# Alternating the first feed forward's up and down slabs, seven block products in 14 of 16 down slabs, weight sums on GpSimd

## The reference, cut to what matters

```python
u = rmsnorm(h, norm_ff_g) @ w1              # (256, 1024) @ (1024, 4096)
h = h + jnp.square(jax.nn.relu(u)) @ w2     # (256, 4096) @ (4096, 1024)
```

## Time and profile before

| What | Value |
|---|---|
| median of 3 runs | 883.88 us (883.88 to 883.88) |
| profiled execution | 884.08 us, span 882.2 us |
| PE busy | 874.6 us, 99% of the span |
| VectorE, ScalarE, GpSimd busy | 647.6, 502.4, 117.9 us |
| granted clock of PE over the span | 1.00 (full speed) |
| HBM read | 158.86 MB, 181 GB/s over the span |

### The profile page before, as it was taken

The page is one execution under the profiler, slowest core; times in us unless marked ns, Lnnn a source line. Parts: engine busy times, 40 slices in busy tenths (PEclk is TensorE's granted clock), DMA queues, the critical chain, the costliest instruction groups (busy, mean ns, idle before and its releaser), DMA issues.

```text
span 882.2 us, 15673 instructions
## 1 busy us (share of the span) xinstructions
PE 874.6 (99%) x6269; PEld 809.7 (92%) x6269; DVE 647.6 (73%) x881; ACT 502.4 (57%) x741; POOL 117.9 (13%) x136
## 2 busy tenths in 40 slices
PE   9999999999999999999999999999999999999997
PEld 9998988989989999888899989999998899999886
DVE  5887987656538887998775548978686788888643
ACT  7786655546547555545473356656634766666432
POOL 5561433000001000000142250001000100000000
PEclk9999999999999999999999999999999999999999
DMA  9969444354535666466556554354556386676641
GB/s 304 319 226 311 164 144 144 104 177 148 172 94 187 195 195 197 160 230 219 191 184 210 191 191 141 104 188 138 174 191 191 105 225 195 194 198 201 192 143 48
DMA packets 137399, 160.67 MB, mean 182 GB/s; under 512 B 4161, under 2 KB 113857, under 8 KB 137089
## 3 DMA queue, kind: packets, MB, share of 16 engines
q1 hardware_dynamic: 135280, 152.83, 54.1%
q0 software_dynamic: 1344, 6.03, 2.0%
q10 hardware_dynamic: 720, 1.06, 0.3%
HBM read 158.86 MB, written 1.05 MB: 181 GB/s over the span
## 4 chain that ended last, share of the span: by engine, by line
PE 98%; issue 1%; ACT 0%; DVE 0%; POOL 0%; DVEq 0%; POOLq 0%; ACTq 0%
PE tb L718 18%; PE tb L719 18%; PE tb L720 18%; PE acc L718 11%; PE acc L720 11%; PE acc L719 11%; PE acc L1043 1%; PE tb L1242 0%; PE tb L1122 0%; PE acc L1272 0%; PE tb L1140 0%; PE acc L1140 0%; PE acc L1290 0%; PE acc L1122 0%; PE tb L1241 0%
## 5 line engine op out<-in xcount | busy, mean ns | idle before, releaser
L1944 DVE TENSOR_TENSOR wlo<-raw,whi 128x2048 fp32r<-128x2048 f32 (+1 forms) x138 | 313.9, 2279 | 118.5 <-ACT whi L1389 117.9
L1389 ACT ACTIVATE whi<-raw 128x2048 fp32r<-128x2048 f32 (+1 forms) x138 | 261.4, 1896 | 140.6 <-PE acc L720 85.2
L718 PE MATMUL tb<-xhi,whi 128*128 128x256 f32 x1192 | 331.8, 278 | 0.2
L719 PE MATMUL tb<-xlo,whi 128*128 128x256 f32 x1192 | 329.5, 276 | 0.0
L720 PE MATMUL tb<-xhi,wlo 128*128 128x256 f32 x1192 | 329.5, 276 | 0.0
L718 PEld LDWEIGHTS tb<-xhi,whi 128*128 128x128 f32 x1192 | 224.1, 188 | 1.1 <-issue 1.0
L719 PEld LDWEIGHTS tb<-xlo,whi 128*128 128x128 f32 x1192 | 224.2, 188 | 0.1
L720 PEld LDWEIGHTS tb<-xhi,wlo 128*128 128x128 f32 x1192 | 224.0, 188 | 0.0
L720 PE MATMUL acc<-whi,xlo 128*128 128x512 f32 x112 | 44.0, 393 | 0.0
L718 PE MATMUL acc<-whi,xhi 128*128 128x512 f32 x112 | 43.8, 392 | 0.0
L719 PE MATMUL acc<-wlo,xhi 128*128 128x512 f32 x112 | 43.8, 391 | 0.0
(11 more groups left out here) (448 smaller groups left out, 1598.2 us busy)
## 6 DMA issues: line engine op xcount, KB each, us to landing
raw<-in_w_in SPq DMA_DIRECT2D x37, 1024.0 KB, 5.2
raw<-in_w SPq DMA_DIRECT2D x26, 1024.0 KB, 5.4
raw<-in_w_up SPq DMA_DIRECT2D x44, 512.0 KB, 5.0
raw<-in_w_down SPq DMA_DIRECT2D x22, 512.0 KB, 4.2
raw<-in_w_xkv SPq DMA_DIRECT2D x8, 1024.0 KB, 5.3
raw<-in_w_out SPq DMA_DIRECT2D x8, 1024.0 KB, 4.9
raw<-in_w SPq DMA_DIRECT2D x12, 512.0 KB, 4.5
raw<-in_w_mem_kv SPq DMA_DIRECT2D x4, 1024.0 KB, 5.2
```

What stands on the lines that cost most here:

```text
L718: pe.matmul(o, a_hi, b_hi, start=start, stop=False)
L719: pe.matmul(o, a_hi, b_lo, start=False, stop=False)
L1389: act.activation(whi[:, n % RING, cut], raw[:, n % RING, cut], ACT.Copy).then_inc(hi_ready, 1)
L1944: dve.tensor_tensor(low(n)[:, cut], raw[:, n % RING, cut], whi[:, n % RING, cut].bitcast(F32), ALU.subtract).then_inc(lo_ready, 1)
```

## The change

The list of slabs alternates: up 0, up 1, down 0, up 2, down 1, and so on to up 15, down 14, down 15. Fourteen of the sixteen down slabs (all but the last two) are done with seven block products. The up slabs write one bank (`acc[:, 1, 1]`). `hid_hi` and `hid_lo` are now rings of three places of 896 columns: four blocks (one of them the difference S3) and the three sums S1, S2, S4. The weight sums are no longer made in `raw` by VectorE but by GpSimd, from `raw` into a tile of their own, `forms`, of two places; ScalarE rounds them (`form_hi`) and VectorE splits them (`form_lo`) in two halves of 128x1024. SP may overwrite a down slab's `raw` when GpSimd has made the sums, where it waited for VectorE's split of them before. At the end ScalarE copies the four gathered products from `tb` to `forms` at once, GpSimd adds them up, and VectorE adds the four results to `h` behind the last slab's activations.

```diff
+    UP = [first["w1"] + max(2 * j - 1, 0) for j in range(16)]
+    DOWN = [first["w1"] + min(2 * j + 2, 31) for j in range(16)]
+    SEVEN = DOWN[:14]
...
                 if n - RING in SEVEN:
-                    sp.wait_ge(sev["lo"], 2 * SEVEN.index(n - RING) + 2)
+                    sp.wait_ge(sev["t"], 2 * SEVEN.index(n - RING) + 2)
...
+            def weight_sums(j):
+                i, n = j, DOWN[j]
+                b12, b11, b21, b22 = (raw_forms(n)[:, s, :] for s in range(4))
+                t3, t1, t2, t4 = (forms[:, i % 2, s, :] for s in range(4))
+                pool.wait_ge(raw_landed[n % RING], landed[n])
+                if i >= 2:
+                    pool.wait_ge(sev["lo"], 2 * i - 2)
+                pool.tensor_tensor(t3, b22, b12, ALU.subtract)
+                pool.tensor_tensor(t1, b12, b11, ALU.subtract).then_inc(sev["t"], 1)
+                pool.wait_ge(sev["t"], 2 * i + 1)
+                link(pool.tensor_tensor(t2, t3, b11, ALU.add))
+                pool.tensor_tensor(t4, b21, t2, ALU.subtract).then_inc(sev["t"], 1)
...
             for j in range(15):
+                emptied(UP[j] if j else first["xo"] + 3)
+                t_slab(UP[j + 1], XHI["h2"], XLO["h2"], None, whole=acc[:, 1, 1, :])
+                if j == 0:
+                    emptied(UP[0])
                 pe.wait_ge(ffn["lo"], j + 1)
...
+                if DOWN[j] in SEVEN:
+                    seven_slab(j)
                 else:
+                    plain_slab(j)
             pe.wait_ge(ffn["lo"], 16)
-            pe.wait_ge(sev["folded"], 1)
-            last_row_slab("x2", hid_hi, hid_lo, 30)
+            pe.wait_ge(sev["kept"], 1)
+            last_row_slab("x2", hidden(hid_hi, 15), hidden(hid_lo, 15), 0)
...
+            form_hi(0, 0)
+            form_hi(0, 1)
+            relu(0)
+            hi(n0 + 3)
+            hidden_hi(0)
+            for j in range(15):
+                if j:
+                    hi(n0 + 2 * j + 3)
+                if DOWN[j + 1] in SEVEN:
+                    form_hi(j + 1, 0)
+                    form_hi(j + 1, 1)
+                elif DOWN[j] not in SEVEN:
+                    act.wait_ge(slab_done, SEVEN[-1] + 1)
+                    act.activation(forms[:, 0, :, :], tb[:, :, :], ACT.Copy).then_inc(sev["kept"], 1)
+                relu(j + 1)
+                hi(n0 + 2 * j + 4)
+                hidden_hi(j + 1)
...
+            square(0)
+            form_lo(0, 0)
+            form_lo(0, 1)
+            lo(n0 + 3)
+            hidden_lo(0)
+            for j in range(15):
+                seven = DOWN[j + 1] in SEVEN
+                if j:
+                    lo(n0 + 2 * j + 3)
+                if seven:
+                    form_lo(j + 1, 0)
+                square(j + 1)
+                if seven:
+                    form_lo(j + 1, 1)
+                lo(n0 + 2 * j + 4)
+                hidden_lo(j + 1)
+            fold()
```

More of the change, by code:

```diff
@@ L36 @@
 RING = 3
+HIDS = 3
 SLAB = 2048
@@ L87, in plan @@
     rows("xo", w["w_xo"], 4)
-    cols("w1", w["w1"], 0, 16)
-    rows("w2", w["w2"], 16)
+    first["w1"] = len(slabs)
+    for kind, j in [("up", 0)] + [s for j in range(15) for s in (("up", j + 1), ("down", j))] + [("down", 15)]:
+        if kind == "up":
+            slabs.append(("T", w["w1"][:, j * 256:(j + 1) * 256].rearrange("(k p) c -> p k c", p=P), 8, 256, "act"))
+        else:
+            ap = w["w2"][j * 256:(j + 1) * 256, :].rearrange("(k p) c -> p k c", p=P)
+            slabs.append(("N", ap, 2, 1024, "dve" if j == 15 else None))
     wi = w["w_in_2"]
@@ L282, in two_blocks @@
         ffn = sems("ffn", "sq hi lo")
-        sev = sems("sev", "t hi lo kept folded")
+        sev = sems("sev", "sums t hi lo kept")
         pl = sems("pl", "ready mm hi lo")
@@ L435, in two_blocks, with hidden, hid_width @@
         turned_x = turned_mem = xn[:, :, :].rearrange("p t c -> p (t c)").rearrange("p (k m) -> p k m", k=KT)
[L437 to L442, removed]
+        def hidden(room, j):
+            return room[:, j % HIDS, 0:512].rearrange("p (k t) -> p k t", k=2)
+        def hid_width(j):
+            return 7 * P if DOWN[j] in SEVEN else 4 * P
         def raw_forms(n):
@@ L514, in _ @@
                 sp.dma_start(fpt[:, 0, 64 * i:64 * i + 64], w[n].broadcast_to([P, 64])).then_inc(lam_in, 16)
-            for n in range(RING + 1, first["w1"]):
+            for n in range(RING + 1, first["cv"]):
                 if n in PIECES:
@@ L667, in _ @@
                            ).then_inc(gfin_in, 16)
+            for j in range(1, len(SEVEN)):
+                weight_sums(j)
+            first_four = forms[:, 0, :, :]
+            q00, q01, q11, q10 = (first_four[:, s, :] for s in range(4))
+            pool.wait_ge(sev["kept"], 1)
+            link(pool.tensor_tensor(q11, q00, q11, ALU.add))
+            link(pool.tensor_tensor(q10, q11, q10, ALU.add))
+            link(pool.tensor_tensor(q11, q11, q01, ALU.add))
+            pool.tensor_tensor(q01, q10, q01, ALU.add).then_inc(sev["sums"], 1)
             gain_fin()
@@ L2337, in forms_lo @@
[L2337 to L2343 removed]
+                w = hid_width(j)
+                dve.tensor_tensor(hid_lo[:, j % HIDS, 0:w], sq[:, 0:w], hid_hi[:, j % HIDS, 0:w].bitcast(F32),
+                                  ALU.subtract).then_inc(ffn["lo"], 1)
```

218 lines of the change are left out of this document (78 added, 140 removed).

## The result

The changed kernel takes 934.64 us (median of 4, 933.23 to 935.46) against 883.88 us: 1.0573 times as long, 95% interval 1.0554 to 1.0591. The forecast was 929 us, in a range of 908 to 952. The profiled execution has a span of 933.2 us, 51.0 us more than before.

The account below looks back on a forecast made before the run. GpSimd and VectorE together were taken as the bound: 13 pairs x 3.0 us over PE = 39.0, + 10 start + 1.5 end - 5.44 removed matmuls = +45.1 us on 883.88, so 929 us; range 908 to 952.

Parts of the forecast that it names:

- PE's price: Matrix engine's time for one up slab and one down slab in the stage: 5.44 + 4.76 = 10.20 us.
- VectorE's price: VectorE's ten instructions for a pair of up and down slab: 9.44 us, which alone fits into 10.20.
- Sharing: GpSimd's and VectorE's instructions in a pair exclude each other, less 0.135 us a handover: 13.2 us, between 12.7 and 14.6.
- New waits: ScalarE's rounding waits for GpSimd's sums, next relu and rounding queue behind, loads wait too; upper bound 14.6 us a pair.
- The loop of load and sums: A slab's load waits for GpSimd's reading, lands in 5.4 us, then four sums; reason for keeping 14.6 us a pair.
- The start: Before the first down slab, now third in order, PE waits about 10 us, at least 6, for its operands.
- rival 1: GpSimd and VectorE don't block each other: pair 10.20 us, start 6.3, end 1, total 886 us; chance 0.07.
- The end: Last down slab's activations and VectorE's adding of four kept products to h: 1.5 us, between 0 and 3.
- Rival 2: First down slab's operands come sooner, start under 3.7 us, so the kernel gets faster: 881.5 us; chance 0.03.
- Rival 3: VectorE keeps the port over several instructions, sums come late, nothing overlaps: 14.6 us a pair, 945 to 950; chance 0.20.
- Rival 4: PE's clock falls in its new waits, 3 us a pair and 10 at the start: over 952 us; chance 0.05.
- The test: Signs in the stage: sums two to three us, down slabs 13 us apart, PE idle before each, busy time down 5 us.

Follow-up runs that it names:

- the kernel with 8-wide memsets: Changed kernel with GpSimd's four weight sums from the third block-product slab on replaced by 8-wide memsets giving the same signals: 893.16 us.

## Why the prediction came out as it did

*The bound, removed, PE's price, VectorE's price.* They hold. Where nothing is in the way the steps are 10.25 us, for 10.20; VectorE's ten instructions add up to 9.42, for 9.44.

*Sharing.* Right in kind. 41.5 of the 51 us hang on GpSimd's sums, and of the 44.5 us by which the thirteen steps exceed PE's price 34 stay when the relu is moved (12.82 less 10.20) and 10 go. The price was read from six rows of another stage, with other operations, and the 0.135 us of a handover there is close to the 0.14 found here. The count was wrong: I let fourteen instructions meet a handover and ten of them save its part, but GpSimd's four can make eight changes at most. VectorE's instructions save another 0.41 us a pair among themselves, with or without GpSimd, and this I had left out. The two errors nearly cancel: with the relu first, the ten steps from the third down slab take 13.19 us, for 13.2. That it came so close is luck.

*New waits.* The prediction named the relu and the next rounding behind ScalarE's wait for GpSimd, and put no price on them but the upper bound. They cost 0.95 us in each of the ten steps. This term, which the forecast put at nothing, is the step that failed: the ten steps take 14.14 us where I had 13.2, together 9.4 more. The first two (13.08 and 10.25) and the last (12.24) are 4.0 shorter than three steps of 13.2. So all thirteen are 5.4 us more than forecast, a mean of 13.62, and that is the distance of the forecast; what the start came out shorter, the end and the unplaced microsecond make up for. "PE waits once in each pair" fell with it: it waits at every second down slab, up to 4.3 us, and ahead of up slabs in between, ended by the relu. I had listed waits that end on the relu as a sign against the forecast; they turned up, as 8.3 of 27.8 us. Long and short steps alternate (15 to 16.5 and 12 to 13 us), and GpSimd does the sums of two slabs close together and then waits for the next load, once 12.2 us. The mean is what counts: without the second slab's sums the third to the eighth step take 13.9 us each, and the mean is 13.61 all the same.

*The loop of load and sums.* Kept as the reason for 14.6. Loads that land 1.6 us sooner shorten the step by 0.37 us; this loop does not set it.

*The start.* 8.8 instead of 10, for the reasons given: 5.6 without sharing, where rival 1 had 6.3, and 3.2 from sharing.

*The end.* 2.2 instead of 1.5: 1.6 for the low half, 0.6 for h.

*Rival 1* (no blocking, 886) is out by the pair of memset and sum: VectorE's 1024-wide subtraction takes 1.219 us beside memsets and up to 2.32 beside sums. The trace is on the side of the page "SBUF — State Buffer" of the Trainium skill (SBUF: two separate sides), which counts in VectorE instructions with two SBUF inputs, and against "Advanced Engine Details and Errata" (VectorE Performance Modes), by whose rule the 1024-wide subtraction would have kept its 1.22 us. *Rival 2* needed a start under 3.7 us; it is 8.8. *Rival 3* (nothing overlaps, 14.6 us) did not come, though single steps of 16 us show the place that it named: VectorE waiting for what waits for GpSimd. *Rival 4*: the clock did fall, at each of the five waits of 3.0 to 4.3 us ahead of down slabs and at the start, and PE's busy time rose by 11.2 us instead of falling by 5, so this sign of the test was wrong. In the loop it cost nothing that can be measured, since the slow slabs lie beside VectorE's work. Of the Trainium skill's rule on waits that bring the clock down in every round ("TensorE: Matmul & The Clock Gate", HAM oscillation) the trace shows the fall, to 0.72 on average from 380 to 390 us, and not the price. At the start there is a price where PE is the bound: 2.4 us in the kernel with 8-wide memsets. In the changed kernel the first step takes 13.08 us for the same reason (granted clock 0.78, PE busy throughout); whether these 2.8 us reach the end isn't shown, since PE waits 3.0 us for VectorE at the fourth down slab.

*The test.* GpSimd's sums were to take two to three microseconds each; the means are 1.54, 1.88, 2.22 and 2.12. VectorE's 2048-wide subtraction beside one came as forecast (3.27 and 3.35, for 3.4), and so did the steps of about 13 us. PE's idle time before each down slab and its fallen busy time did not.

About 1 us of the 51 is left without a place.

## To carry over

Before work is moved to an engine that is idle, look in the trace for a stretch where both engines have work queued: if their instructions stretch to each other's length there, they count as one, and a move is worth it only if the new engine does the work faster; here it took 1.285 us for what VectorE does in 0.692. Put a wait for the helper behind everything in its queue that others need: one relu on the wrong side of such a wait, with the square that hangs on it, cost 8.6 us. A lower clock and a long idle time in the profile are not shown to be a loss until an experiment that takes them away makes the kernel faster.

## What the runs showed of the hardware that I had not expected

An instruction of GpSimd with a single SBUF input excludes VectorE as one with two does (0.945 us alone, up to 2.87 beside it), and a memset, which reads nothing, doesn't: 48 memsets beside a VectorE that was busy 85% of the time took 1.233 to 1.247 us. The page "SBUF — State Buffer" of the Trainium skill (SBUF: two separate sides) says of VectorE's instructions with two SBUF inputs that they take the shared pair only against a GpSimd operation that reads SBUF; both runs agree. Ahead of the stage the changed kernel's trace also has the other side, an instruction of VectorE with one input in SBUF and the other in PSUM (`acc`):

```profile
269.04 1.29 POOL L678 TENSOR_TENSOR forms<-raw 128x512 f32<-128x512 f32 x1 [51.49 <-PE acc L752]
269.07 0.68 DVE L2026 TENSOR_TENSOR h<-acc,h 128x512 f32<-128x512 f32 x1
```

It takes 0.68 us under GpSimd's sum, as it does at 267.24 with GpSimd idle, and the sum its 1.29. Neither holds the other.

The turn does not always pass after one instruction. In the earlier trace rows several of VectorE go ahead of one of GpSimd; with the relu first, one of VectorE's of 0.29 us took 3.00 behind two of GpSimd.

Two engines that exclude each other still lose little at the changes: about 0.14 us is saved at each. With the relu moved, 9.42 and 5.14 us of instructions take 13.19 us a pair, of which 0.13 us VectorE is idle.
